# One decoder layer on eight cores: from channel-major 256-token tiles to token-major 512-token tiles

## The reference

```python
u = h @ w_mix_in                                   # 1024 -> 2560: B, C, v | GLU value, GLU gate
y_a = b_a * causal_dwconv(c_a * v_a, conv_a_w)     # width 3, 512 channels
z = glu_v * sigmoid(glu_g)
z = causal_dwconv(z, conv_b_w) + conv_b_b          # width 31, 512 channels
y_b = silu(layernorm(z, ln_b_g, ln_b_b))
mix = concat([y_a, y_b]) @ w_mix_out
# cross-attention, 4 heads of 256, into 256 memory tokens
p = softmax(q @ k.T / 16);  o = (p @ v) @ w_o      # q = h @ w_q, k, v = mem_n @ w_k, w_v
# feed-forward, hidden 2816
ffn = (silu(h @ w_gate) * (h @ w_up)) @ w_down
x = x + rmsnorm(sublayer(rmsnorm(x, g_pre)), g_post)   # three times
```

## Time and profile before

| | before |
|---|---|
| timed runs, slowest core | 1091.15 us median of 3 (1090.78 to 1095.68) |
| profiled execution, span of the slowest core | 1091.1 us |
| span of the other cores | 1080.7 to 1088.7 us |
| PE busy | 1011.1 us, 93% |
| DVE, ACT, POOL busy | 410.0, 438.2, 183.1 us |
| moved by DMA | 98.82 MB |

### The profile page before, as it was taken

How to read it: one execution, slowest core, us unless ns; L and a number is a source line. 1 busy time by engine, 2 the same in 40 slices (tenths; PEclk the granted TensorE clock), 3 DMA queues, 4 the chain that set the end, 5 groups by cost and what they waited for, 6 DMA issues and landing times.

```text
span 1091.1 us, 23597 instructions; the slowest of 8 cores (1080.7 to 1091.1 us)
## 1 busy us (share of the span) xinstructions
PE 1011.1 (93%) x9040; PEld 872.8 (80%) x9040; DVE 410.0 (38%) x948; ACT 438.2 (40%) x1016; POOL 183.1 (17%) x271
## 2 busy tenths in 40 slices
PE   1899999999999789999998999999999999999994
PEld 1788888888888577888885888888888888888884
DVE  8254644634545423344444212222222212222212
ACT  2234354353443646566655224142423324141312
POOL 7001020220221322232244102020202002020201
PEclk9899999999999889999999999999999999999998
DMA  9999700000002985920082943333432433333431
GB/s 157 183 141 119 205 2 2 2 1 2 1 2 48 162 140 92 161 30 2 2 105 41 165 117 109 105 126 102 128 102 88 146 107 120 108 122 100 133 98 49
DMA packets 74174, 98.82 MB, mean 91 GB/s; under 512 B 26704, under 2 KB 42320, under 8 KB 73584
## 3 DMA queue, kind: packets, MB, share of 16 engines
q0 software_dynamic: 33680, 35.26, 23.4%
q1 hardware_dynamic: 40384, 62.05, 19.1%
HBM read 121.94 MB, written 14.16 MB: 125 GB/s over the span
## 4 chain that ended last, share of the span: by engine, by line
PE 77%; DVE 6%; ACT 6%; DMA 5%; issue 4%; POOL 2%; DVEq 0%; ACTq 0%; POOLq 0%
PE ps L408 45%; PE ps L852 14%; PE ps L571 10%; DMA t<-w_mix_in 3%; DMA t<-w_q 2%; DVE t L437 2%; ACT t L417 2%; POOL t L442 2%; PE ps L753 1%; PE ps L383 1%; PE ps L422 1%; PE ps L773 1%; DVE t L535 1%; ACT L427 1%; PE ps L876 1%
## 5 line engine op out<-in xcount | busy, mean ns | idle before, releaser
L408 PE MATMUL ps<-t,t 128*128 128x256 bf16 (+1 forms) x5824 | 684.2, 273 | 26.1 <-DVE t L396 8.3
L408 PEld LDWEIGHTS ps<-t,t 128*128 128x128 bf16 x5824 | 562.5, 99 | 105.8 <-issue 34.2
L442 POOL TENSOR_TENSOR t<-t,t 128x256 f32<-128x256 f32 x188 | 132.1, 727 | 828.1 <-DVE t L437 825.7
L491 DVE TENSOR_TENSOR t<-ps,t 128x256 bf16<-128x256 f32 x176 | 73.8, 424 | 333.9 <-ACT t L488 333.9
L488 ACT ACTIVATE t<-ps 128x256 f32<-128x256 f32 x176 | 67.2, 387 | 299.7 <-PE ps L408 262.3
L852 PE MATMUL ps<-t,t 128*128 128x256 bf16 x1408 | 181.5, 274 | 3.6 <-DVE t L437 3.6
L437 DVE SCALAR_TENSOR_TENSOR t<-ps,t,t 128x256 f32<-128x256 f32 x192 | 88.4, 481 | 188.4 <-ACT t L429 155.9
L852 PEld LDWEIGHTS ps<-t,t 128*128 128x128 bf16 x1408 | 137.7, 98 | 22.7 <-issue 6.3
L571 PE MATMUL ps<-t,t 128*128 128x256 bf16 x992 | 112.5, 272 | 0.0
L571 PEld LDWEIGHTS ps<-t,t 128*128 128x128 bf16 x992 | 96.2, 97 | 12.4
L417 ACT ACTIVATE t<-ps 128x256 bf16<-128x256 f32 x192 | 67.7, 394 | 93.0 <-PE ps L408 68.3
(11 more groups left out here) (71 smaller groups left out, 481.5 us busy)
## 6 DMA issues: line engine op xcount, KB each, us to landing
t<-wd_bf SPq DMA_DIRECT2D x176, 256.0 KB, 2.7
outT<-t SPq DMA_DIRECT2D x7, 1024.0 KB, 5.7
t<-xT SPq DMA_DIRECT2D x6, 1024.0 KB, 47.5
wd_bf<-w_down POOLq DMA_DIRECT2D x22, 256.0 KB, 76.6
t<-w_gate POOLq DMA_DIRECT2D x2, 2816.0 KB, 31.0
t<-w_up POOLq DMA_DIRECT2D x22, 256.0 KB, 12.1
t<-w_mix_in POOLq DMA_DIRECT2D x4, 1024.0 KB, 24.1
t<-xT POOLq DMA_DIRECT2D x2, 1024.0 KB, 25.3
```

Source lines behind the costliest of these rows:

```text
L408: S.op("pe", (lambda kc=kc, i=i: lambda e: e.matmul(hb(dst_bank, dst_half, n), lhsT=lhs_fn(kc), rhs=rhs_fn(kc), start=(i == 0), stop=(i == ...
L442: S.op("dve" if (last and oc % 2 == 1) else "pool", (lambda oc=oc, xs=xs: lambda e: e.tensor_tensor(out=xs(), in0=xs(), in1=tb[:, oc % nt, ...
L491: S.op("dve", (lambda j=j, b=b: lambda e: e.tensor_tensor(out=actj[:, j % 4, :], in0=hb(b, 1), in1=sg[:, j % 2, :], op=ALU.mult))(), reads ...
```

## The change

The program is written anew. What it does:

- **Layout.** x comes and goes token-major, 128 tokens on the partitions and 1,024 channels along the free dimension, in blocks of 128. Tiles are 512 tokens (`TT = 512`, 4 tiles of 4 blocks). The tokens of a tile are permuted on the host: row r of a block group holds tokens of phase r mod 8 (`P = 8`, `TAU = 64`).
- **RMSNorm.** Per token, so the sum runs along the free dimension: one ACT square with `accum_out`, two one-column POOL operations (`finish_rstd`), one DVE scale (`pre_block`, `post`).
- **Transposes.** The normed block is turned channel-major by a DMA transpose on SP's queue (`dmaT`), 67 of them in all: before the input projection, for the memory tokens, before attention (`h2load`, from DRAM), of the softmax output (`scores`) and before the FFN (`pre3`). x after each sub-layer goes to DRAM (`x1`, `x2`) and is loaded again.
- **Convolution, width 31.** Blocks of 16 channels x 8 phases fill the 128 partitions; 5 banded 128 x 128 matrices (`wconv`, built on chip by `build_wc`) per block do the convolution with matmuls of 64 columns. To get to that layout and back the data goes through DRAM (`zbounce`, `conv`).
- **Attention.** `Am` = Wq K^T (scaled) and `Bm` = V Wo are made once. Scores are one product h Am per block, the output one product P Bm. The softmax subtracts a maximum, and sums in the exp.
- **FFN.** All gate, up and down weights are in SBUF by the start of the stage. They are loaded during the end of stage 1 and during attention, by POOL's queue.

```diff
-TT = 256
+TT = 512
+P = 8
+TAU = TT // P
...
-                    for k in range(31):
-                        di = 12 + k * 4 + c
-                        S.op("pe", (lambda c=c, k=k, di=di, b=b, hf=hf, par=par: lambda e: e.matmul(
-                            hb(b, hf), lhsT=diag[:, di, :], rhs=zbuf[:, par, c, 2 + k:2 + k + TT],
-                            start=(k == 0), stop=(k == 30)))(),
...
+        def zbounce(t):
+            pr = t % 2
+            dma("sp", "zst", zd[pr].rearrange("(q p) s t -> p q (s t)", p=128),
+                zst[:, :, :, :].rearrange("p q s t -> p q (s t)"), zkeys, ["zd%d" % pr])
+            src = zd[pr].rearrange("(g c) s t -> s c g t", c=GC)
+            S.dmas("sp", "zp", [(lambda s: lambda e: e.dma_start(out=zp[s * GC:(s + 1) * GC, :, :], in_=src[s]))(s)
+                                for s in range(P)], ["zd%d" % pr], ["zp"])
+        def conv(t):
+            for h in range(2):
+                pt, bk = pair()
+                for gg in range(16):
+                    g = h * 16 + gg
+                    for d in range(ND):
+                        mm(pt[:, gg * TAU:(gg + 1) * TAU], wconv[:, g * ND + d, :], zp[:, g, HT - d:HT - d + TAU],
...
+            dma("sp", "zcp", cd[pr], zcp[:, :, :], ["zcp0", "zcp1"], ["cd%d" % pr])
+            src = cd[pr].rearrange("(r c) (q g) t -> g c q r t", c=GC, q=4)
+            S.dmas("sp", "zc", [(lambda g: lambda e: e.dma_start(
+                out=zc[g * GC:(g + 1) * GC, :, :].rearrange("c q (r t) -> c q r t", r=P), in_=src[g]))(g)
+                for g in range(8)], ["cd%d" % pr], ["zc"])
...
+        wload("pool", "wq", wqT[:], wq_d, ["wq"])
+        wload("pool", "wo", wo[:], wo_d, ["wo"])
+        kv(wk, "wk", KT, "KT")
+        xres = [load_x(x_d[(NT - 1) * 4 + b]) for b in range(4)]
+        for j in (18, 19):
+            wload("pool", "gu%d" % j, wgu[:, j], wgu_d[:, j], ["gu%d" % j])
+        ln_stats()
+        ln_math()
+        kv(wv, "wv", VT, "VT")
...
+        def scores(B):
...
+            dmaT("pT%d" % s, pT[:, s, :, :], pb[:, s, :], ["p%d" % s], ["pT%d" % s])
...
+        for i in range(NB + LAG):
+            if i < NB:
+                xsl[i] = load_x(x1_d[i], ["x1_%d" % i])
+                scores(i)
+            if i % 4 == 3 and i // 4 + 2 < NT:
+                h2load(i // 4 + 2)
+            if i >= LAG:
+                attn_out(i - LAG, xsl[i - LAG])
+                flush(1)
...
+            for _ in range(2):
+                if wq_list:
+                    j = wq_list.pop(0)
+                    wload("pool", "gu%d" % j, wgu[:, j], wgu_d[:, j], ["gu%d" % j])
```

More of the change, by code:

```diff
@@ L52, in __init__, with place @@
         self.nrec = 0
-        self.cur = ""
+        self.range = {}
+        self.over = {}
         for e in ENGS:
             self.sems[e] = stack.enter_context(nc.semaphore("s_" + e))
+    def place(self, key, lo, hi, group=None):
+        assert key not in self.range, key
+        self.over[key] = []
+        for k2, (l2, h2, g2) in self.range.items():
+            if lo < h2 and l2 < hi and (group is None or g2 != group):
+                self.over[key].append(k2)
+                self.over[k2].append(key)
+        self.range[key] = (lo, hi, group)
     def dma_sem(self, name):
@@ L69, in _deps @@
                 toks.append(st["w"])
[L70 to L75, removed]
+        for k0 in writes:
+            for k in [k0] + self.over.get(k0, []):
+                st = self.bufs.get(k)
+                if st:
+                    if st["w"] is not None:
+                        toks.append(st["w"])
+                    toks.extend(st["r"].items())
         need = {}
@@ L166, in body @@
             def body(e):
-                for (waits, fn, inc, _lbl) in lists[engname]:
+                for (waits, fn, inc) in lists[engname]:
                     for (sk, v) in waits:
@@ new lines @@
+    small[:, SM_LNB:SM_LNB + 4] = f(ln_b_b).reshape(4, 128).T
+    small[:, SM_G2:SM_G2 + 8] = f(xa_pre_g).reshape(8, 128).T
+    small[:, SM_MASK:SM_MASK + GC] = np.tile(np.eye(GC, dtype=np.float32), (P, 1))
+    wsm = np.zeros((P, GC, NG, ND, P), np.float32)
+    for s in range(P):
+        for r in range(P):
+            for d in range(ND):
+                lag = r - s + P * d
+                if 0 <= lag <= 30:
+                    wsm[s, :, :, d, r] = cbw[30 - lag].reshape(NG, GC).T
+    wsm = wsm.reshape(128, NG * ND * P)
@@ new lines @@
+    gains = np.stack([np.broadcast_to(f(g)[None, :], (128, D)) for g in
+                      (mix_pre_g, mix_post_g, mem_norm_g, xa_post_g, ffn_pre_g, ffn_post_g)])
+    kmaj = lambda w: c_(f(w).reshape(-1, 128, w.shape[1]).transpose(1, 0, 2))
+    wi = kmaj(w_mix_in).reshape(128, 8, 5, 4, 128)
+    bb, cc, vv, gv, gg = (wi[:, :, i] for i in range(5))
+    units = [np.concatenate([gg[:, :, c], gv[:, :, c]], axis=2) for c in range(4)]
+    units += [np.concatenate([cc[:, :, c], vv[:, :, c]], axis=2) for c in range(4)]
```

1300 lines of the change are left out of this document (566 added, 734 removed).

## The result

The changed kernel takes 1191.91 us (median of 4 runs, 1178.86 to 1259.47) against 1091.74 us (median of 4, 1090.78 to 1095.68). The ratio is 1.083, 95% interval 1.0782 to 1.0878: 8% slower, where 960 us was forecast, outside the range of 890 to 1045. The profiled execution took 1178.86 us, its span is 1177.2 us.

What follows compares the result with a forecast made beforehand. The kernel was taken as bound by the number of matmuls times their pitch. 824 us of matmuls plus waits of 38, 10, 8, 49, 15, 7, 5 and 9 gave 965, stated as 960 us, range 890 to 1045.

Steps and rivals of the forecast that it cites:

- The count of matmuls and their price: TensorE over the whole kernel: 4,544 matmuls, 3,584 of them of 512 columns at 0.216 us, sum 824 us, 160 less than before.
- the clock falls: Rival: denser matmuls on all eight cores lower the granted clock to 0.88 or 0.78; whole 1070 to 1190 us; chance 0.06.
- The 49 us wait before the last LayerNorm sums: End of stage 1: tile 3's convolution trip back is held up by POOL's weight stream; largest single loss, 49 us.
- The end: After the last matmuls: square, scale, add and a 512 KB store, 9 us.
- Tile 0's 10 us: Stage 1, first tile: convolution's trip out, caught in the weight stream, lands near 86 us; PE gets there at 76.
- The transposes appear in no row. ... I take the first: DMA transposes, all stages: taken as 4 KB pieces, under 1 us plus about 2 of landing, not as 256-byte rows.
- a sign of being wrong: Profile after: transposes landing in over 10 us would show the forecast wrong.
- transposes come as 256-byte rows: Rival: start +28 us, attention +50 us while weights come; 1035 us, range 995 to 1080; chance 0.17.
- 10 + 8 us: Stage 1's tiles: 10 us for tile 0's trip out, 8 for three convolution trips back, each short by about 2.5.
- None becomes the bound: DVE, ACT and POOL in stage 1 and attention: less time than PE per tile or block, except DVE in tile 0.
- 38, 10, 8, 49, 15, 7, 5, 9: Idle PE, us: start, tile 0's trip, trips back, stage 1's end, attention's weight stream, softmax chain, FFN crumbs, end.
- they alternate one for one: DMA engines beside a weight stream: each small SP packet costs a whole cast packet, some 0.4 us for 4 KB rows.

Runs made afterwards that it cites:

- e1: Changed kernel with POOL's w_q load, and all weight loads behind it, held until the last convolution result has landed; ratio 1.0955 to the kernel before.
- e6b: Changed kernel with every 128-row DMA transpose replaced by a plain copy in 2 KB pieces, output not the reference; ratio 1.0433 to the kernel before.
- e5: Changed kernel with the add to x behind stage 1's output projection moved from POOL to DVE; ratio 1.0573 to the kernel before.
- e10: Changed kernel with start transposes ahead of gated weight loads, add on DVE and lists reordered, later weight stream unchanged; ratio 0.9976 to the kernel before.
- e7_zcone: Changed kernel with the convolution's way back from DRAM in 4 KB instead of 128-byte pieces, output not the reference; ratio 1.0724 to the kernel before.

## Why the prediction was wrong

**Right.** The bound before. The count of matmuls and their price: 824 forecast, some 822 at full clock. The convolution is cheaper still (31.6 ns where 39 was chosen of 27 to 109.7). The FFN's matmuls take 458 us where 456 + 5 was said, at a granted clock of 0.99: the rival *the clock falls* did not come. The Trainium skill's limiter of 13/16 for dense matmuls (TensorE: Matmul & The Clock Gate, Part 1) does not show in the profiled execution: from 704 to 1155 us each of the eight cores was granted 0.99 or 1.00 of the clock while TensorE was 98 to 100% busy. The 49 us wait before the last LayerNorm sums was right in place, releaser and cause (e1 takes the stream away and 41 of its 59 us go). The end: 8 us for 9. Tile 0's 10 us came true by luck: PE waited 11.2 us there, but for DVE, none of it for the trip.

**The step that failed: "The transposes appear in no row. ... I take the first".** That is, pieces of 4 KB instead of 1,024 rows of 256 bytes, between ends of 3 us and 26 us each. Beside the first stream the five issues hold SP's queue for 40.4 us, between 1.2 and 27.7 each, and their median landing is 11.7 us, over the 10 that the forecast had named as a sign of being wrong. The packets are these (all queues from 22 to 67 us):

```profile
DMA packets 4950, 7.30 MB, mean 162 GB/s; under 512 B 3632, under 2 KB 3632, under 8 KB 4694
...
q0 software_dynamic: 1494, 6.45, 83.0%
q1 hardware_dynamic: 3456, 0.85, 14.0%
```

3,456 packets with 0.85 MB are 246 bytes each. This was the rival *transposes come as 256-byte rows*, chance 0.17, with the right places (start and attention) and 1035 us, itself 143 us short. Its sizes: +28 us at the start (measured 69.08 for 38, +31) and +50 in attention (measured 95.6 us of waits from 505 to 711 us and at its end, for 22 forecast, +74). e6b shows that larger pieces get back only some 43 us of it.

**What no step had: order.** The prediction costed engines by their busy time and each wait by the transfer it waits for. It named what was queued behind the waiting instruction for PE alone. Stage 1's tiles were to wait 10 + 8 us; they wait 71.6 (sum of PE's brackets from 69 to 379 us). Their releasers are ACT and DVE, not DMA: ACT behind squares of x not yet loaded (8.56, at 234 us), behind the memory tokens (17.32), DVE in tile 0 (8.58), and the chain of scale, add, square and root, 6.2 us per block. *"None becomes the bound"* was true of shares (21 to 30%) and false of the chain. e5 shows the chain's 28 us; e10 shows 93 for order, start and add together, with every transfer still there and the later weight streams as they were.

**Sums.** PE without a matmul was forecast at 141 us (38, 10, 8, 49, 15, 7, 5, 9) and is 322.5: +31 at the start, +54 in stage 1, +26 from 379 to 505 us (74.5 for 49), +74 in attention; the end is 8.0 and the small gaps are 3.7 where 14 were allowed, -2. The matmuls add +31 (-2 for their pitch, +33 put down to half clock after waits, a term the sum lacked). That is 212 us with the rounding, which is 1177 less the sum of 965.

**Still open.** Whether all of the 33 us are half clock, and how they divide over the waits, since no run removed waits and kept all else. What reordering the lists is worth by itself, and whether a second queue for the transposes or the trips would have spared the rest: neither was run. And the order of service between the queues: "they alternate one for one" does not hold for the small packets.

## What to carry to other kernels

A rewrite that removes TensorE work gains it only where TensorE stays the bound; for every new transfer and every step of a norm, write down what stands ahead of it in its own queue, and what stands behind it, before its price. Small-packet DMAs and a cast stream on another queue should not meet: gate or pace the stream, but check where it goes instead, since e1 shows the same loss come back 100 us later. Order is the better first try: here order, the gated start and the moved add gave 93 us together, pacing 20 on top, and a gate or pacing alone 13 or less. And read a merged line of a queue with care: 45 us for five transposes held 40 of issuing, 17.67 us for four copies held 2.

## What the runs showed of the hardware

- A DMA transpose of a 128 x 1024 bf16 block is 256-byte packets. In quiet it costs 1.23 us of SP's issue and lands in 2.7 us (the last one of the start, at 65.92); beside a cast stream the issues took 1.3 to 27.7 us, and SP issued nothing else meanwhile. The Trainium skill puts a DMA transpose at 261 GB/s (DMA: Bandwidth & Descriptors, Latency and other measured facts); by that figure one is 1.0 us, an estimate. The nearest here is the 1.23 us of issue.
- In e6b_copy2k plain copies of the same 256 KB in 2 KB pieces took 0.47 to 0.54 us of issue beside the cast stream, but landed after 9.2 to 15.0 us.
- From 388 to 431 us POOL's queue moved 1,134 packets and SP's 2,671: 2.4 small ones to a cast packet, not one for one. In e7_zcone, with 4 KB pieces, it was close to one for one (815 to 812 from 388 to 431 us). By the Trainium skill's rule (DMA: Bandwidth & Descriptors, Queues, rings and completion order) an engine drains a whole packet, typically of some 9 to 17 descriptors, before it turns to the next queue. Whether a packet of this profile is one of those no run here shows, so the first ratio does not refute the rule and the second does not prove it.
- Behind long waits TensorE's 512-column matmuls ran at 468 ns (4 in 1.87 us behind the wait of 17.32) and 453 ns (6 in 2.72 us behind 13.19), twice the 217 ns of the FFN, with a granted clock of 0.51 (the 1.2 GHz level) over the hole from 379 to 435 us.
- A one-column POOL operation with a power takes 0.55 to 0.84 us in the block of tile 1 above, a 1024-column float32 add on POOL 2.34 us.
